# An expert layer's opening is reordered, and its shared down matrix moves behind round 0

## The reference, cut to what matters

```python
def swiglu(x, wg, wu, wd):
    return (jax.nn.silu(x @ wg) * (x @ wu)) @ wd

scores = jax.nn.sigmoid(x @ w_router)          # 264 x 64
...                                            # the best 8 of the best 4 groups of 8
routed = jnp.zeros_like(x).at[tok_s].add(ybuf[dest] * w_s[:, None])
shared = swiglu(x, ws_gate, ws_up, ws_down)    # 1024 -> 256 -> 1024
return routed + shared
```

## Time and profile before

| | us |
|---|---|
| median of 3 runs | 1641.63 (1640.94 to 1641.82) |
| span of the profiled execution | 1639.0 |
| expert layer 0: round 0 starts, round 1 starts | 406.84, 433.75 |
| expert layer 1: round 0 starts, round 1 starts | 1122.11, 1149.78 |
| TensorE busy | 1542.3 (94%) |

### The profile page before, as it was taken

One profiled execution on the slowest core, in us unless ns is written; L12 is line 12 of the kernel. 1 busy time (PEld: TensorE's weight loads), 2 busy tenths in 40 slices (PEclk: granted clock), 3 DMA queues, 4 the chain that ended last, 5 costly groups with the idle time before them and its releaser, 6 DMA issues. The chain is left out here.

```text
span 1639.0 us, 29881 instructions
## 1 busy us (share of the span) xinstructions
PE 1542.3 (94%) x11300; PEld 1034.8 (63%) x11300; DVE 734.1 (45%) x2034; ACT 372.5 (23%) x784; POOL 96.3 (6%) x121
## 2 busy tenths in 40 slices
PE   6999989998999999999999899998999999999996
PEld 4778765776655655665565587766565566566553
DVE  3205435226464445345345335354745434533445
ACT  2002443113121121122111245332112112111122
POOL 0000100001000000000000001010000000000000
PEclk9999999999999999999999999999999999999998
DMA  9996799337999999999899783986999999998994
GB/s 366 386 371 245 291 397 388 110 129 323 376 420 420 420 420 420 419 419 418 344 390 416 245 267 122 375 320 259 419 420 421 420 420 421 418 418 342 378 420 187
DMA packets 150665, 580.21 MB, mean 354 GB/s; under 512 B 17341, under 2 KB 62561, under 8 KB 101290
## 3 DMA queue, kind: packets, MB, share of 16 engines
q1 hardware_dynamic: 134442, 535.74, 82.4%
q0 software_dynamic: 15488, 40.92, 6.5%
q10 hardware_dynamic: 640, 2.26, 0.3%
HBM read 568.22 MB, written 26.90 MB: 363 GB/s over the span
## 5 line engine op out<-in xcount | busy, mean ns | idle before, releaser
L2391 PE MATMUL ps<-ring,scratch 128*64 128x256 f32 x3840 | 428.5, 383 | 17.7 <-DMA ring<-in_moe_w_up 16.4
L2391 PEld LDWEIGHTS ps<-ring,scratch 128*64 128x64 f32 x3840 | 289.7, 138 | 143.6 <-issue 26.9
L2439 PE MATMUL ps<-ring,scratch 128*64 128x512 f32 x960 | 214.7, 597 | 0.2 <-DVE scratch L2837 0.2
L2352 PE MATMUL ps<-scratch 128*128 128x264 bf16 x1488 | 183.1, 277 | 5.2 <-issue 4.3
L2776 DVE SCALAR_TENSOR_TENSOR scratch<-scratch,ps 128x256 f32<-128x256 f32 x64 | 30.8, 481 | 348.5 <-ACT scratch L2929 341.6
L697 PE MATMUL ps<-hT,ring 128*128 128x264 f32 x768 | 180.5, 389 | 1.3 <-ACT hT L379 1.3
L2352 PEld LDWEIGHTS ps<-scratch 128*128 128x128 bf16 x1488 | 131.3, 97 | 57.8 <-issue 19.6
L697 PEld LDWEIGHTS ps<-hT,ring 128*128 128x128 f32 x768 | 146.0, 192 | 30.7 <-issue 2.5
L2439 PEld LDWEIGHTS ps<-ring,scratch 128*64 128x64 f32 x960 | 62.4, 136 | 126.2 <-issue 93.3
L2743 DVE TENSOR_TENSOR scratch<-scratch,ps 128x264 f32<-128x264 f32 x240 | 103.4, 431 | 76.7 <-PE ps L2352 76.4
L2929 ACT ACTIVATE scratch<-ps 128x256 f32<-128x256 f32 x64 | 24.6, 385 | 441.2 <-PE ps L2391 421.5
(11 more groups left out here) (403 smaller groups left out, 1376.2 us busy)
## 6 DMA issues: line engine op xcount, KB each, us to landing
ring<-in_moe_w_gate SPq DMA_DIRECT2D x128, 1024.0 KB, 17.6
ring<-in_moe_w_up SPq DMA_DIRECT2D x128, 1024.0 KB, 17.6
ring<-in_moe_w_down SPq DMA_DIRECT2D x128, 1024.0 KB, 18.2
ring<-in_ada_w SPq DMA_DIRECT2D x48, 1024.0 KB, 13.7
ring<-in_ret_w_in SPq DMA_DIRECT2D x24, 1024.0 KB, 16.9
ring<-in_state_ret SPq DMA_DIRECT2D x16, 1024.0 KB, 14.6
out_ret_sample<-ring POOLq DMA_DIRECT2D x16, 1024.0 KB, 9.1
ring<-in_gla_w_in SPq DMA_DIRECT2D x12, 1024.0 KB, 13.3
```

The lines of the kernel that those rows point to most:

```text
L2352: mm = nc.tensor.matmul(k.ps[:, c % 2, 0:T], parts_of(p)[:, s, c * P:(c + 1) * P], slot_token[:, p, :], start=(p == 0 and s == 0), stop=(p ...
L2391: mm = nc.tensor.matmul(k.ps[lo:lo + CAP, 2 + p, j * DE:(j + 1) * DE], xg[:, p, c, lo:lo + CAP], slot(k, n, DE)[:, c, :], start=(c == 0), ...
L2439: mm = nc.tensor.matmul(k.ps[lo:lo + CAP, 6 + half, :], hid_t[:, p, m, lo:lo + CAP], slot(k, n, D)[:, m, half * 512:(half + 1) * 512], sta ...
```

## The change

1. The shared down matrix leaves the front of the layer's loads and is loaded after the 12 loads of round 0. Everything behind it moves one place forward in the ring; `place` takes one off for round 0.
2. Its products (now `shared_down`) move from before the first gather to the end of round 0, in banks 2, 3, 0, 1. ScalarE's copies of them (`acc`) move behind its round 0.
3. The token-major transposes go behind the score transposes, in two pairs of banks (`TOKEN_BANK`), so that the second doesn't wait for the copy of the first; the third goes behind two of the eight chunks of the shared gate product. ScalarE copies the third one out before the first SiLU.
4. The rank matmuls go between chunks of the shared expert's second gate product, and `list_rows` for round 0 right behind four more chunks. VectorE writes the row numbers out before it computes the weights.
5. The first gather comes right after the shared up products. The row numbers of round 1 (`list_rows(pe, 1)`) move from before round 0 to behind the products of its first pair of experts.
6. VectorE's `list_order` is cut in two: `find_special` runs before the shared hidden values, the rest (now `list_order`) and `next_slots(1)` after `take` of round 0.
7. `sh_hid` lies in the spare area of `hT` instead of in `scratch`.

```diff
     def moe(layer):
...
+        for w in shared[0:2]:
+            plan.append((what, w))
         for r in range(ROUNDS):
             for name, e in ROUND:
                 plan.append((f"moe{layer}", ...))
+            if r == 0:
+                plan.append((f"shared_down{layer}", shared[2]))
...
         @block.sync
-            load_until(k, sp, n_sh + 3 + RING)
+            load_until(k, sp, n_shd + 1)
             sp.wait_ge(s_count, 1)
...
         def pe_round(pe, r, late=0):
...
+                if first and p == 0:
+                    list_rows(pe, 1)
...
+            if first:
+                shared_down(pe)
             if not isinstance(r, int) or r + 2 <= LAST:
                 list_rows(pe, r + 2)
+        def shared_down(pe):
+            wait_slot(k, pe, n_shd)
+            w = slot(k, n_shd, D)
+            pe.wait_ge(g_even, 2 * PAIRS)
+            pe.wait_ge(g_odd, 2 * PAIRS)
+            for c in range(DC):
+                if c >= 4:
+                    pe.wait_ge(s_shx, c - 3)
+                for m in range(FC):
+                    mm = nc.tensor.matmul(...)
+                mm.then_inc(s_shd if c < DC - 1 else k.ring_free[n_shd % RING], 1)
+            pe.wait_ge(s_shx, DC)
...
         @block.tensor
             mm.then_inc(s_log, 1)
-            token_major(0, *TOKENS[0])
             pe.wait_ge(s_frow, 1)
             cond_transpose(k, k.ps[:, 2], fill_rows).then_inc(s_fcrt, 1)
             pe.wait_ge(s_sig, 1)
...
             mm.then_inc(s_sc, 1)
-            token_major(1, *TOKENS[1])
+            token_major(0, *TOKENS[0], bank=TOKEN_BANK[0])
+            token_major(1, *TOKENS[1], bank=TOKEN_BANK[1])
             wait_slot(k, pe, n_sh)
             pe.wait_ge(s_fmod, 1)
-            shared(0, 0, range(DC)).then_inc(s_shg, 1)
-            token_major(2, *TOKENS[2])
-            shared(0, 1, range(DC)).then_inc(k.ring_free[n_sh % RING], 1)
+            shared(0, 0, range(2))
+            pe.wait_ge(s_natc, 1)
+            token_major(2, *TOKENS[2], bank=TOKEN_BANK[2])
+            shared(0, 0, range(2, DC)).then_inc(s_shg, 1)
+            shared(0, 1, range(2))
             pe.wait_ge(s_ch, 1)
...
             mm.then_inc(s_rk, 1)
+            shared(0, 1, range(2, 6))
+            pe.wait_ge(s_natc, TT)
+            list_rows(pe, 0, bank=6)
+            shared(0, 1, range(6, DC)).then_inc(k.ring_free[n_sh % RING], 1)
             wait_slot(k, pe, n_sh + 1)
             shared(1, 0, range(DC))
-            pe.wait_ge(s_natc, TT)
-            list_rows(pe, 0, bank=6)
             shared(1, 1, range(DC)).then_inc(k.ring_free[(n_sh + 1) % RING], 1)
+            pe.wait_ge(s_idxc, 1)
+            pe.wait_ge(s_got, 16 * PAIRS)
+            gather_tile(pe, 0, 0)
+            pe.wait_ge(s_shh, FC)
+            gather_tile(pe, 1, 0)
             pe.wait_ge(s_eye, 1 + 3 * (PAIRS + 1))
             pe.wait_ge(s_w0, 1)
-            pe.wait_ge(s_shh, FC)
             slots_first(pe)
-
-            wait_slot(k, pe, n_sh + 2)
...
-            gather(pe, 0)
-
-            pe.wait_ge(s_shx, DC)
-            list_rows(pe, 1, bank=6)
             pe_round(pe, 0)
...
         @block.vector
+            v.wait_ge(s_idx, 1)
+            row_numbers(PAIRS, bank=6, to=first_rows_at).then_inc(s_idxc, 1)
             link(nc.vector.tensor_tensor(weight, score, chosen, ALU.mult))
             link(nc.vector.tensor_reduce(total, weight, AX.X, ALU.add))
-            v.wait_ge(s_idx, 1)
-            row_numbers(PAIRS, bank=6, to=first_rows_at).then_inc(s_idxc, 1)
...
+            find_special(v)
             wait_used(k, v, n_sh + 1)
...
             v.sem_inc(s_add, DC)
+            take(v, 0, 0, nc.vector.tensor_copy, g_even)
             list_order(v)
             next_slots(1, [expert_at(v, EPI + e) for e in range(EPI)])
-            take(v, 0, 0, nc.vector.tensor_copy, g_even)
             v.wait_ge(s_idx, 2)
-            row_numbers(PAIRS, bank=6).then_inc(s_idxc, 1)
+            row_numbers(PAIRS).then_inc(s_idxc, 1)
             round_(0)
...
         @block.scalar
+            take(act, 0, 1, nc.scalar.copy, g_odd)
+            round_(0)
             for c in range(DC):
                 if c < DC - 1:
                     act.wait_ge(s_shd, c + 1)
                 else:
-                    wait_used(k, act, n_sh + 2)
+                    wait_used(k, act, n_shd)
                 nc.scalar.copy(acc[:, c, :], k.ps[:, DOWN_BANK[c % 4], 0:T]).then_inc(s_shx, 1)
-            take(act, 0, 1, nc.scalar.copy, g_odd)
-            round_(0)
```

More of the change, by code:

```diff
@@ L223, in moe @@
         what = f"shared{layer}"
-        for name in ("sh_w_gate", "sh_w_up", "sh_w_down"):
-            w = inp[name][layer]
-            plan.append((what, w.rearrange("(k p) n -> p k n", p=P)))
+        shared = [inp[name][layer].rearrange("(k p) n -> p k n", p=P) for name in ("sh_w_gate", "sh_w_up", "sh_w_down")]
+        for w in shared[0:2]:
+            plan.append((what, w))
         for r in range(ROUNDS):
@@ L2019, in experts @@
     sh_silu = sc[:, at[0]:at[0] + FC * T].rearrange("p (m t) -> p m t", m=FC)
-    sh_hid = sc[:, at[0] + FC * T:at[0] + 2 * FC * T].rearrange("p (m t) -> p m t", m=FC)
+    sh_hid = spare[:, 0:FC * T].rearrange("p (m t) -> p m t", m=FC)
     silu = area((PAIRS + 1) * DE).rearrange("p (b f) -> p b f", b=PAIRS + 1)
@@ L2080, in experts @@
     fill = k.places["ada"][4 * FILL[layer]:4 * FILL[layer] + 4]
-    n_sh, n_moe = k.stage[f"shared{layer}"], k.stage[f"moe{layer}"]
+    n_sh, n_moe, n_shd = k.stage[f"shared{layer}"], k.stage[f"moe{layer}"] + 1, k.stage[f"shared_down{layer}"]
     n_end = n_moe + ROUNDS * RING
@@ L2124, in hidden_chunk, with place @@
         return hid[:, p, :].rearrange("p (q m) -> p m q", m=FC)[:, m, :]
-    def place(kind, e, of=PLACE):
-        return n_moe + of[(kind, e)]
+    def place(kind, e, of=PLACE, r=None):
+        return n_moe + of[(kind, e)] - int(isinstance(r, int) and r == 0)
     XSTEPS = 11
@@ L2274, in list_rows, with gather_tile @@
             mm.then_inc(s_idx, 1)
[L2276 to L2282, removed]
+        def gather_tile(pe, p, d):
+            for b in range(2):
+                if p:
                     pe.wait_ge(g_odd if b else g_even, d + p)
@@ L2287, in gather @@
                 mm.then_inc(s_gat, 1)
+        def gather(pe, r, late=0):
+            d = done_tiles(r, late)
+            pe.wait_ge(s_got, 16 * (d + tiles(r)))
+            for p in range(tiles(r)):
+                gather_tile(pe, p, d)
         def spread_slots(pe, p):
@@ L2384, in pe_round @@
                     for name in ("moe_w_gate", "moe_w_up"):
-                        n = place(name, e)
+                        n = place(name, e, r=r)
                         pe.wait_ge(k.ring_full[n % RING], 16 * (r + n // RING + 1))
@@ L2389, in pe_round @@
                         for e in (2 * p, 2 * p + 1):
-                            n, lo = place(name, e), CAP * (e % 2)
+                            n, lo = place(name, e, r=r), CAP * (e % 2)
                             mm = nc.tensor.matmul(k.ps[lo:lo + CAP, 2 + p, j * DE:(j + 1) * DE],
@@ L2430, in pe_round @@
                 for e in (2 * p, 2 * p + 1):
-                    n = place("moe_w_down", e)
+                    n = place("moe_w_down", e, r=r)
                     pe.wait_ge(k.ring_full[n % RING], 16 * (r + n // RING + 1))
@@ L2437, in pe_round @@
                         for e in (2 * p, 2 * p + 1):
[L2438 removed]
+                            n, lo = place("moe_w_down", e, r=r), CAP * (e % 2)
                             mm = nc.tensor.matmul(k.ps[lo:lo + CAP, 6 + half, :], hid_t[:, p, m, lo:lo + CAP],
@@ L2562, in weights_of, with take_tile @@
             return nc.vector.tensor_copy(to, w_parts[:, :, bass.ds(e, 1), :].rearrange("p t o s -> p t (o s)"))
+        def take_tile(eng, p, b, copy, sem, d):
+            eng.wait_ge(s_gat, 2 * d + 2 * p + b + 1)
+            copy(xg_of(p)[:, 4 * b:4 * b + 4, :].rearrange("p c n -> p (c n)"), k.ps[:, b, :]).then_inc(sem, 1)
         def take(eng, r, b, copy, sem, late=0):
             for p in range(tiles(r)):
-                eng.wait_ge(s_gat, 2 * done_tiles(r, late) + 2 * p + b + 1)
-                copy(xg_of(p)[:, 4 * b:4 * b + 4, :].rearrange("p c n -> p (c n)"), k.ps[:, b, :]).then_inc(sem, 1)
+                take_tile(eng, p, b, copy, sem, done_tiles(r, late))
         def last_of(kind, r, p):
@@ L2572, in last_of @@
                 return place(kind, EPI - 1, LIGHT_PLACE)
-            return place(kind, 2 * p + 1 if p < PAIRS else HEAVY_BLOCKS[-1][0])
+            return place(kind, 2 * p + 1 if p < PAIRS else HEAVY_BLOCKS[-1][0], r=r)
         def rows_done(eng, r, p, half, d):
@@ L2583, in rows_done, with find_special @@
                 eng.wait_ge(k.ring_free[n % RING], r + n // RING + 1)
-        def list_order(v):
+        def find_special(v):
             link = lambda ins: k.dve.link(v, ins)
@@ L2601, in list_order @@
```

(2 more changed lines are left out.)

27 lines of the change are left out of this document (10 added, 17 removed).

## The result

The changed kernel takes 1655.46 us (median of 4 runs, 1653.82 to 1657.21) where the kernel before takes 1641.66: a ratio of 1.0081, 95% interval 1.0067 to 1.0095. The sign of the forecast was right. Its size was not: +13.8 us instead of +3.6, and 1655.46 lies above the range's upper end of 1651. The profiled execution took 1657.21 us, its span 1655.3, against a span of 1639.0 before.

The account below looks back on a forecast made before the run. Loads bound each layer after an opening bound by something else. Round 1 starting 6.9 us later, less 5.1 absorbed, leaves 1.8 per layer, +3.6 in two (1.5 to 1.8 in layer 1): 1645.2 us, range 1636 to 1651.

Parts of the forecast that it names:

- First fetch: GpSimd's fetch for round 0's gather: starts at 389.4, limited by the h_rows stores, lands at 399.0; reordering the routing buys 0.
- Start of round 0: TensorE idles 6.7 us, then gathers at half clock for 1.3 more; round 0 starts at 403.6, 3.2 earlier.
- the second fetch: Fetch for round 1's gather, issued inside round 0: lands after 8.3 us, so TensorE waits 2.5 us.
- S: The start of round 0, from which the prediction counts times; round 1 was put at S + 37.0.
- cross-check: TensorE's opening, same work: 11.9 us of waits and slow clock against about 3.5 + 0.95 + 0.6 + 1.6 before.
- inner range: The forecast's own range, 1640 to 1651: clock cost 0 to 1.9 and second wait 0.5 to 4.5 per layer.
- What the loads absorb: Load stream after round 0: dry once, then full, absorbing 5.1 of 6.9 us; 1.8 remain per layer.
- B: Start of round 1 counted from its layer's logits; in layer 0 measured 64.4 before and 75.1 after.
- The fourth: Rival: DMA not as far ahead, loads absorb less, at most all of 6.9 per layer, 1655.4; chance 0.05.
- The first: Rival: second fetch quick, no wait of 2.5 before the second gather, -0.7 per layer, 1640.2; chance 0.15.
- the third: Rival: both fetches land in 3.3 us, no slow clock, -6.7 per layer, 1628.2; chance 0.08.
- the second: Rival: stores no limit, round 0's fetch lands at 395.0, -2.2 per layer, 1637.2; chance 0.12.

Follow-up runs that it names:

- e4: Changed kernel with the shared down matrix and its products back before round 0 and round 1's list early again, only the reordered routing kept: 1633.41 us, ratio 0.9949.
- e3: Changed kernel with round 1's list and fetch made before round 0 again, the down matrix still behind round 0: 1643.62 us, ratio 1.0009.
- e2: Kernel before with only the shared down matrix and products moved behind round 0, and what that needs: 1652.59 us, ratio 1.0079.
- f2: Changed kernel with 15 useless products ahead of the first gather and 10 ahead of the second: 1655.88 us, ratio 1.0095.
- f3: Changed kernel with SyncE holding back all loads of round 1 until the second fetch has landed: 1660.69 us, ratio 1.0116.
- g2: The early-list kernel e3 with the shared down products moved from the end of round 0 to just ahead of the second gather: 1650.14 us, ratio 1.0049.
- g1: The changed kernel measured once more, as a control: 1657.97 us, ratio 1.0099.
- f1: Changed kernel with 15 useless products on TensorE ahead of the first gather: 1658.84 us, ratio 1.0112.
- e1: Changed kernel with the shared down matrix loaded and multiplied before round 0 again, reordering and late list kept: 1640.07 us, ratio 0.9983.

## Why the prediction was right in sign and wrong in size

**First fetch: right.** It was put at 389.4 with the stores as the limit, and GpSimd started at 389.89, released by the store. It landed after 7.6 instead of 8.0, at 399.2. The reordering bought nothing there. But "all of the reordering buys 0" looked at the first fetch alone. In e4, where the down products stand between row numbers and gather, it is worth 0.51%. With the down matrix moved it is worth 0.70%, e3 against e2: in e2 the second gather waits 3.15 us for VectorE's list work, in e3 it doesn't. Which of its steps gives how much was not tried, nor what it is worth beside the late list.

**Start of round 0: right.** 403.90 against 403.6; TensorE idle 7.43 us, gather at half clock (3.90 us), at the 1.3 us that was charged for it (f2).

**Round 0: the second fetch, the term that was mis-sized most.** The list came as reckoned, round 0's second pair at 411.64 (S + 7.7) instead of S + 8.3. GpSimd issued at S + 8.8 and S + 10.1. But where I took 8.3 us to landing, out of rows between 4.2 and 10.3, the pair took 9.5 and 11.3: a wait of 5.0 and not 2.5. The rows had the nearest case, the pair issued beside running loads in 430:460, at 8.5 to 10.3; a mean over unlike cases was the wrong choice. Behind this wait the clock had fallen too, which the sum had counted for the first wait alone: the 16 transposes took 3.53 us where 8 and 8 take 2.5 at full clock. Round 1 came 10.7 us later counted from the logits, not 6.9; in layer 1 10.2, not 6.6. The prediction's own cross-check didn't close either: waits and slow clock of 11.9 against 3.5 + 0.95 + 0.6 + 1.6 = 6.65 make 5.2, not 6.9. And the lower end of its inner range, by the terms it names, is 1.8 - 1.3 - 2.0 per layer, 1638.6 and not 1640.

**What the loads absorb: the second step that failed.** I had "the stream has run dry once, and from there it is full", and so 5.1 us absorbed. The profile after shows three holes behind the first. The one at 430: the shared down load and seven more are issued by 419.93; the next, one slot further on than before, now needs a slot that comes free with round 0's first down products, and goes out at 432.74, as the engines run dry. The other two can be dated the same way: the last load of round 1 goes out near 443.8, when the shared down's slot is free, and the next at 448.39; and none goes out between 459.55 and 471.31, a gap as long as one of the kernel before (448.75 to 460.49) that made no hole there. The prediction followed the last load of round 1 and the first down load of round 2, and not the loads between. In layer 0, 10.7 less 7.1 (8.8 without the 1.7 of clock) is 3.6 absorbed, in layer 1 10.2 less 6.0 is 4.2. Thus per layer +7.1 and +6.0 where +1.8 stood. With the measured B and my 5.1 it would have been +5.6 and +5.1, so some three quarters of the miss is the later round 1 (3.8 and 3.6) and the rest the absorption (1.5 and 0.9). This split follows the prediction's sum; f3, where round 1 starts 5.9 us sooner for nothing, shows that the two terms are not independent. That the waits in rounds 5 to 8 would shrink was right: the first now comes in round 9. (Before, too, not every round from 5 on waited: layer 0's round 7 did not.)

**Rivals.** The fourth ("the loads absorb less, at most all of 6.9, 1655.4"), given 0.05, names the time that came, but with the wrong half of the cause, since its 6.9 was itself 10.7. The first (quick second fetch) and the third are excluded by the landings, the second by GpSimd's start at 389.89, released by a store. By the Trainium skill (DMA: Bandwidth & Descriptors, the anatomy of one DMA) a DMA issued by GpSimd takes about 2.0 us fixed plus its bytes at 436 GB/s, which makes an estimate of 3.2 us for such a fetch. The second fetches of e3 and f3, without loads beside them, come near it (3.2 to 4.2); the changed kernel's in layer 0, 7.5 to 11.3 beside loads, do not.

## What to carry to other kernels

As far as this case goes: where a stream of loads through a ring bounds the kernel, price a change at the opening by the bytes that the stream moves in the next hundred microseconds, and follow every load to the slot that it waits for: work that only moves from behind a slot's release to before it costs time, 0.40% in g2, where no engine shows a wait. Products that look movable may be the cover of a fetch and of VectorE's list work at once. A fetch that shares its queues with a full stream should be priced by the slowest row of that kind, and sent while the stream is dry if it can be.

## What the runs showed of the hardware

The granted clock fell behind waits much shorter than the 6.19 us of the earlier trace rows. In round 12 of layer 0 of the changed kernel, TensorE waits 2.02 us for a load and is then granted 0.50 (1.2 GHz) for a while; the block of 64 products takes 8.81 us instead of 7.13:

```profile
793.07 8.81 PE L2398 MATMUL ps<-ring,scratch 128*64 128x256 f32 x64 [2.02 <-DMA ring<-in_moe_w_up]
```

and in stretches of 2 us around it, where the clock is the third number from the end:

```profile
791.00:793.00 2.00, 0.04 (x2) 0.00 (x0) 0.48 (x1) 0.38 (x1) 0.00 (x0) 1.00 1.00 414
793.00:795.00 2.00, 1.94 (x12) 1.51 (x14) 0.00 (x0) 0.00 (x0) 0.00 (x0) 0.65 0.95 383
795.00:797.00 2.00, 2.00 (x12) 1.38 (x11) 0.00 (x0) 0.00 (x0) 0.00 (x0) 0.50 0.82 340
```

It doesn't follow from the wait alone. In g1, which is the same program, the same block stayed at full speed:

```profile
796.22 7.13 PE L2398 MATMUL ps<-ring,scratch 128*64 128x256 f32 x64 [2.01 <-DMA ring<-in_moe_w_up]
```

A wait of 1.99 us there gave 7.13 us in e3 and 8.81 in f1.

The same kernel's executions spread by some microseconds (1632.59 to 1644.42 in 12 runs of e1). Part of the spread of one execution against another is there before the first expert layer: the logits of layer 0 start at 366.13 us in f2's trace and at 375.31 in e3's, although all that stands ahead of them is the same program. That is why the table has its last column. Why it differs was not tried; in 240 to 280 us the granted clock is 1.00 in f2 and 0.91 in e3.
